# Late adaLN modulation by column groups with row-tile weight loads, and the shared expert's rows added on GpSimd at the end

## The reference, cut to what matters

```python
mod = silu(c) @ w_ada + b_ada                     # c: 1 + 8 conditioning rows; w_ada: 1024 x 6144
sh1, sc1, g1, sh2, sc2, g2 = split(mod, 6)
h = rms(x, norm_pre_mix) * (1 + sc1) + sh1
mix = concat(retention heads, gated-linear-attention (GLA) heads) @ w_out
x = x + g1 * rms(mix, norm_post_mix)
h = rms(x, norm_pre_ffn) * (1 + sc2) + sh2
f = routed_experts(h) + shared_expert(h)          # 64 experts, top 8 per token; one shared expert
y = x + g2 * rms(f, norm_post_ffn)
```

## Time and profile before

| | us |
|---|---|
| median of 3 runs (1336.25 to 1337.11) | 1336.88 |
| the profiled execution's own time | 1338.04 |
| its span, first to last instruction | 1335.8 |

### The profile page before, as it was taken

The page is one execution under the profiler, slowest core; times in us unless marked ns, Lnnn a source line. Parts: engine busy times, 40 slices in busy tenths (PEclk is TensorE's granted clock), DMA queues, the critical chain, the costliest instruction groups (busy, mean ns, idle before and its releaser), DMA issues.

```text
span 1335.8 us, 18616 instructions
## 1 busy us (share of the span) xinstructions
PE 1207.8 (90%) x5990; PEld 828.7 (62%) x5990; DVE 887.0 (66%) x1362; ACT 601.3 (45%) x712; POOL 163.4 (12%) x184
## 2 busy tenths in 40 slices
PE   5899999896899999999999999999999999999810
PEld 0799999754334244444777777777777777777500
DVE  0711442245465357575788888888888888888888
ACT  1422222203221012222677767767767767767501
POOL 0100000000011001101112212212212211221002
PEclk7799999986899999999999999999999999999955
DMA  9332221505135631537999999999999999999896
GB/s 372 138 112 74 74 74 37 130 0 189 63 126 170 230 129 39 142 119 264 355 380 395 389 383 385 378 376 382 375 369 374 377 378 381 374 379 359 348 318 221
DMA packets 91519, 339.20 MB, mean 254 GB/s; under 512 B 12312, under 2 KB 35880, under 8 KB 65420
## 3 DMA queue, kind: packets, MB, share of 16 engines
q1 hardware_dynamic: 75104, 301.02, 61.5%
q0 software_dynamic: 16384, 37.78, 8.1%
HBM read 317.24 MB, written 42.48 MB: 269 GB/s over the span
## 4 chain that ended last, share of the span: by engine, by line
PE 81%; DMA 8%; DVE 7%; ACT 2%; SPq 1%; issue 1%; DVEq 0%; POOLq 0%; POOL 0%; ACTq 0%
PE ps L1650 14%; PE ps L2033 13%; PE ps L2017 8%; PE ps L2013 7%; PE ps L2015 7%; PE ps L2014 7%; PE ps L1999 4%; PE ps L1863 4%; PE ps L1681 3%; DMA arena<-in_w_ada 3%; DMA arena<-expert_rows 2%; PE ps L1891 2%; PE ps L1912 1%; PE ps L1990 1%; PE ps L2023 1%
## 5 line engine op out<-in xcount | busy, mean ns | idle before, releaser
L1493 DVE TENSOR_TENSOR gu_lo<-w_gu,gu_hi 128x1536 fp32r<-128x1536 f32 x128 | 224.4, 1754 | 0.9 <-ACT gu_hi L1011 0.9
L1011 ACT ACTIVATE gu_hi<-w_gu 128x1536 fp32r<-128x1536 f32 x128 | 189.9, 1483 | 0.0
L1488 DVE TENSOR_TENSOR down_lo<-arena,down_hi 128x2048 fp32r<-128x2048 f32 x64 | 146.7, 2293 | 38.5 <-ACT down_hi L1017 38.5
L2013 PE MATMUL ps<-gu_hi,xT_hi 128*112 128x512 f32 x384 | 156.8, 408 | 0.9 <-issue 0.9
L2015 PE MATMUL ps<-gu_hi,xT_lo 128*112 128x512 f32 x384 | 151.2, 394 | 0.0
L2014 PE MATMUL ps<-gu_lo,xT_hi 128*112 128x512 f32 x384 | 150.8, 393 | 0.0
L1650 PE MATMUL ps<-w_hi,hT_hi 128*128 128x300 f32 (+1 forms) x480 | 145.0, 302 | 1.0 <-DVE w_lo L1093 1.0
L1650 PE MATMUL ps<-w_lo,hT_hi 128*128 128x300 f32 (+1 forms) x480 | 144.6, 301 | 0.0
L1650 PE MATMUL ps<-w_hi,hT_lo 128*128 128x300 f32 (+1 forms) x480 | 144.5, 301 | 0.0
L1017 ACT ACTIVATE down_hi<-arena 128x2048 fp32r<-128x2048 f32 x64 | 122.0, 1906 | 2.2 <-DMA arena<-in_w_exp_down 1.9
L2017 PE MATMUL ps<-w_gu,arena 128*112 128x512 f32 x256 | 120.2, 592 | 0.0
(11 more groups left out here) (271 smaller groups left out, 1932.1 us busy)
## 6 DMA issues: line engine op xcount, KB each, us to landing
w_gu<-in_w_exp_gate SPq DMA_DIRECT2D x64, 1024.0 KB, 10.3
w_gu<-in_w_exp_up SPq DMA_DIRECT2D x64, 1024.0 KB, 17.5
arena<-in_w_exp_down SPq DMA_DIRECT2D x64, 1024.0 KB, 12.7
arena<-in_w_ada SPq DMA_DIRECT2D x24, 1024.0 KB, 7.6
arena<-in_w_in SPq DMA_DIRECT2D x12, 1200.0 KB, 5.4
arena<-expert_rows SPq DMA_DIRECT2D x9, 1024.0 KB, 13.3
arena<-expert_rows SPq DMA_DIRECT2D x4, 2048.0 KB, 11.3
arena<-in_x_prompt SPq DMA_DIRECT2D x8, 512.0 KB, 8.7
```

The costliest lines, as they stand in the source:

```text
L1011: a.activation(gu_hi[b % RING][:, :, ks], w_gu[b % U][:, :, ks], ACT.Copy).then_inc(s_ghi, 1)
L1488: v.tensor_tensor(down_lo[:, :, :], w_dn[b % RING], down_hi[:, :, :].bitcast(F32), ALU.subtract).then_inc(s_dlo, 1)
L1493: v.tensor_tensor(gu_lo[b % U][:, :, ks], w_gu[b % U][:, :, ks], gu_hi[b % RING][:, :, ks].bitcast(F32), ALU.subtract).then_inc(s_glo, 1)
L2013: pe.matmul(out, x_hi, gu_hi[r][:, :, k], start=(k == 0), stop=False)
```

## The change

- The late modulation is tiled like the early one. Load `i` (0 to 15) brings row tile `k = i % 8` of half `g = i // 8`: 128 rows x 2048 columns, 8 KB a row. Four matmuls (`mod_piece`) write four column groups of one bank; the bias is four more matmuls a half. PE does 3, 3, 2, 3 and 3 pieces in the turns of the GLA loop and the last two behind it. Piece 8 waits until the first half has been folded.
- DVE folds twice, each time with two instructions of 64 partitions x 512: half 0 at the start of turn 3, half 1 behind the loop, ahead of `heads(PT)`. `mod_rows` becomes 256 rows x 512, and the loads back are in rows of 512 values. For each sample sequence there are two loads where there was one.
- `w_mod2` no longer uses the region ST0, and loads 2 and 3 don't wait for the store of the retention state.
- `w_out` is loaded in four parts. Row tiles 0, 1 and 6 (1.5 MB) are issued after the GLA states are stored, the others (2.5 MB) when the last GLA output has been copied. All `w_ada` loads are issued ahead of both.
- At the end DVE's addition of the shared rows is removed from `middle_ranks`. GpSimd does it, after the last scatter has landed and after `s_bcg`, and DVE waits for it ahead of its last addition.

```diff
-        w_mod2 = [region(at, 4, 512) for at in (MOD0 + 4 * D, HT0, HT0 + 2 * D, ST0)]
-        mod2 = region(MOD0, 8, 512, rows=NCOND)
+        w_mod2 = [region(at, 4, 512) for at in (MOD0 + 2 * D, MOD0 + 4 * D, HT0, HT0 + 2 * D)]
+        mod2 = region(MOD0, 2, 512)
+        MOD2_TURNS = (3, 3, 2, 3, 3)
...
+            def store_mod2(g):
+                sp.wait_ge(s_fold, 3 + g)
+                sp.dma_start(mod_rows[g * P:(g + 1) * P, :], mod2[:, g]).then_inc(s_mst, 16)
...
-            for i in range(1, 13):
+            for i in range(2, 12):
                 load_mod2(i)
+            store_mod2(0)
+            sp.wait_ge(s_out, 16)
+            sp.wait_ge(s_mst, 16)
+            sp.dma_start(bc2[:, 0:2]..., mod_row[0, 0:1].broadcast_to([P, 4, 512])).then_inc(s_bc2, 16)
+            for i in range(12, 16):
+                load_mod2(i)
             sp.wait_ge(s_sg, NCH)
...
+            load_w_out(0, 2)
+            load_w_out(6, 1)
             sp.wait_ge(s_goe, NT)
             sp.wait_ge(s_out, 16 * (1 + H))
-            sp.dma_start(w_out_buf, w_out[0].rearrange("(k p) n -> p k n", p=P)).then_inc(s_wout, 16)
-            for i in range(14, 16):
-                load_mod2(i)
+            load_w_out(2, 4)
+            load_w_out(7, 1)
+            store_mod2(1)
...
+            g.wait_ge(s_bcg, 16 * (1 + SB + 2))
+            for n, t in enumerate(LAST_ORDER):
+                R = ROWS[t]
+                g.wait_ge(s_add, t + 1)
+                g.tensor_tensor(ffn_sum[t][0:R], ffn_sum[t][0:R], shared[0:R, t], ALU.add).then_inc(s_tick, 1)
...
-                step(v.tensor_tensor(to, to, shared[0:R, t], ALU.add))
                 v.wait_ge(s_yb[t], 32)
                 step(v.tensor_tensor(y[:, 0], y[:, 0], y[:, 1], ALU.add))
+                v.wait_ge(s_tick, 1 + (done - NT))
                 mark(v.tensor_tensor(to, to, y[:, 0], ALU.add), s_add, done)
...
+            def mod_piece():
+                i = mod_pieces[0]
+                mod_pieces[0] += 1
+                g, k = i // KT, i % KT
+                pe.wait_ge(s_wada[i % 4], 16 * (i // 4 + 3))
+                if i == KT:
+                    pe.wait_ge(s_fold, 3)
+                for c in range(4):
+                    o = pe.matmul(ps[c * CG:c * CG + NCOND, MOD2_BANK], condT[:, k, :], w_mod2[i % 4][:, c], start=(k == 0), stop=False)
+                o.then_inc(s_ada, 1)
+                if k == KT - 1:
+                    pe.wait_ge(s_rows, 16 * 12)
+                    for c in range(4):
+                        o = pe.matmul(ps[c * CG:c * CG + NCOND, MOD2_BANK], K("selp")[c * CG:c * CG + 1, 0:NCOND], mod2_bias[c * CG:c * CG + 1, g],
+                                      start=False, stop=True)
+                    o.then_inc(s_mod, 1)
...
-            pe.wait_ge(s_fold, 2 + 5)
-            mod_mm(5)
-            mod_mm(6)
-            pe.wait_ge(s_goe, NT)
-            mod_mm(7)
+            while mod_pieces[0] < 2 * KT:
+                mod_piece()
```

More of the change, by code:

```diff
@@ L236, in hybrid_step @@
         mod1_bias = region(ST0 + 2 * D, 4, 512, rows=1)
[L237 to L240 removed]
+        w_mod2 = [region(at, 4, 512) for at in (MOD0 + 2 * D, MOD0 + 4 * D, HT0, HT0 + 2 * D)]
+        mod2 = region(MOD0, 2, 512)
+        mod2_bias = region(MOD0 + D, 2, 512)
+        MOD2_BANK = 2
+        MOD2_TURNS = (3, 3, 2, 3, 3)
         condT = sb("condT", [P, KT, NCOND])
@@ L551, in _ @@
                              state_gla[0, :, h].rearrange("b d v -> d b v")).then_inc(s_st, 16)
[L553 to L556, removed]
+            for c in range(4):
+                sp.dma_start(mod2_bias[c * CG:c * CG + 1], b_ada[0:1, 2 * D:6 * D].rearrange("a (g c n) -> a g c n", g=2, c=4)[:, :, c])\
+                    .then_inc(s_rows, 16)
+            for g, c, w in ((0, 0, norm_post_mix), (1, 0, norm_pre_ffn), (1, 2, norm_post_ffn)):
+                for half in range(2):
+                    sp.dma_start(mod2[(c + half) * CG:(c + half + 1) * CG, g], w[0:1, half * 512:half * 512 + 512].broadcast_to([CG, 512]))\
+                        .then_inc(s_rows, 16)
             def load_mod2(i):
@@ L1127, in _, with mod_fold @@
             v.wait_ge(s_const, 32)
[L1129 to L1134, removed]
-                    mark(v.tensor_copy(m, raw), s_fold, n + 3)
+            def mod_fold(g):
+                v.wait_ge(s_mod, g + 2)
+                v.wait_ge(s_rows, 16 * 12)
+                first, last = slice(0, 2 * CG), slice(2 * CG, P)
+                step(v.scalar_tensor_tensor(out=mod2[first, g], in0=ps[first, MOD2_BANK], scalar=float(g), in1=mod2[first, g], op0=ALU.add, op1=ALU.mult))
+                if g == 0:
+                    mark(v.tensor_copy(mod2[last, g], ps[last, MOD2_BANK]), s_fold, 3)
                 else:
-                    mark(v.scalar_tensor_tensor(out=m, in0=raw, scalar=one, in1=m, op0=ALU.add, op1=ALU.mult), s_fold, n + 3)
+                    mark(v.scalar_tensor_tensor(out=mod2[last, g], in0=ps[last, MOD2_BANK], scalar=0.0, in1=mod2[last, g], op0=ALU.add, op1=ALU.mult), s_fold, 4)
             def rotate(t):
@@ L1312, in _ @@
                     heads(t - 1)
-            mod_fold(4)
             head_squares(PT)
+            mod_fold(1)
             v_of_state(0)
             heads(PT)
-            for n in range(5, 8):
-                mod_fold(n)
             v.wait_ge(s_go, NT)
@@ L1802, in _ @@
                         o.then_inc(s_kv, 1)
-                        mod_part(t, 1 + c)
-                    mod_part(t, 3)
-                else:
-                    mod_part(t, 1)
-                    mod_part(t, 2)
-                    mod_part(t, 3)
+                        if c < MOD2_TURNS[t] - 1:
+                            mod_piece()
+                else:
+                    for n in range(MOD2_TURNS[t] - 1):
+                        mod_piece()
                 pe.wait_ge(s_gp, t + 1)
```

69 lines of the change are left out of this document (29 added, 40 removed).

## The result

The changed kernel takes 1319.33 us, the median of 4 runs (1313.46 to 1323.16), against 1336.57 us for the kernel before (4 runs): ratio 0.988, 95% interval 0.985 to 0.991. It is 17 us faster; 31 were forecast. The time lies at the upper end of the whole range (1295 to 1320) and outside the forecast's own (1300 to 1312), at the time of the rival "the clock stays low" (1320). The profiled execution took 1323.16 us, the longest of the four: span 1321.3, mean granted clock 0.920. The shortest, 1313.46, had 0.929. Medians and ranges here leave out three executions that took over 1.5% longer than the shortest of their kernel: 1599.03 of the kernel before, 1345.64 and 1348.22 of e10_fill_64_rows.

The account below looks back on a forecast made before the run. The chain of waits through PE and ACT, with modulation on it, was taken to bound the GLA loop and the gap behind. -16 - 21.6 + 1.7 + 1 + 4.1 = -30.8 from 1338.0 gave 1307.2, median 1306; range 1300 to 1312, whole 1295 to 1320.

Parts of the forecast that it names:

- the clock stays low: Rival, GLA loop: with modulation gone, PE's short matmuls and waits keep the clock low; 1320 us, chance 0.13.
- What one piece costs: Late modulation on PE: a piece of 8 records takes 1.07 us, or 1.94 at low clock, against 3.53 before.
- groups in series: Rival, modulation: four 9-column groups run one after another, a piece costs 3.53 us; 1346 if unhidden, chance 0.05.
- Turn by turn, -16: GLA loop: five turns save 4.7, 4, 3, 1 and 3.8 us, sum -16, range -20 to -11.
- The clock: GLA loop and behind: less modulation may leave more at 1.2 GHz; taken off in turns 1 and 2, 1.7 us added behind.
- Turn 3: GLA loop: PE sheds 3.5 us, but piece 8 waits for DVE's fold behind `heads(1)`; only 1 kept.
- The loads of `w_ada` don't decide: GLA loop: each load is asked for four pieces ahead, loads 12 to 15 a turn before they are needed.
- Behind the loop, -21.6: Last output copy to first output projection: 31.3 us become 9.6, with `w_out` the last to arrive; -21.6.
- The clock behind the loop, +1.7: Output projection: starting after a wait of some 2.7 us, it runs partly at low clock; +1.7 us.
- Loads back, +1: Samples' rows loaded back in 16 DMAs, not 8: between 2.7 us worse and 2 saved, taken as +1.
- The end: Final additions: GpSimd's five at 2.5 us go in turn with DVE's ten; +4.1 us, range -2.5 to +17.

Follow-up runs that it names:

- e10_fill_64_rows: Changed kernel plus zero-weight filler matmuls at 13 places, each four matmuls in four column groups, on 64 rows of PE: 1332.06 us, ratio 0.995.
- e3_fill: Changed kernel plus 13 zero-weight matmuls in one column group, two per GLA turn and three more ahead of the last outputs: 1310.82 us, ratio 0.982.
- e5: Changed kernel with 14 of the 16 modulation pieces written to column group 0 alone, so their matmuls run serially: 1321.68 us, ratio 0.989.
- e4: Changed kernel with `w_ada` loads 12 to 15 issued ahead of the modulation store and the 1 MB `bc2` load: 1323.44 us, ratio 0.988.
- e1: Changed kernel with the shared expert's rows added by DVE at the end, as before the change, not GpSimd: 1320.33 us, ratio 0.986.
- e7: Changed kernel plus zero-weight filler at 13 places, each four matmuls in four column groups, on 128 rows: 1310.06 us, ratio 0.981.
- e11: e7 with the shared expert's rows added by DVE at the end, as before the change: 1310.51 us, ratio 0.980.

## Why the prediction was wrong, point by point

**What one piece costs: right.** 1.05 or 1.89 us. The rival of groups in series is out.

**Turn by turn, -16: wrong, +4.0.** (The five terms make -16.5.) By turn, turn 0 from the first transposes to the first copy, the others copy to copy:

| turn | forecast | changed kernel | e3_fill |
|---|---|---|---|
| 0 | -4.7 | +0.9 | -2.6 |
| 1 | -4 | -1.9 | -6.8 |
| 2 | -3 | +1.4 | -4.8 |
| 3 | -1 | -2.0 | +2.5 |
| 4 | -3.8 | +5.5 | -1.9 |

Counted on a full clock the sum was right to 2 to 4 us (73 forecast; 75.4 and 76.7 with filler, which holds some of it itself). That is in part luck: the turns of e3 lie up to 3.5 off, in both directions. (In turn 2 the working leaves out the bias of the first half, which stands with piece 7 between the state products, so nothing was uncovered there.) What failed is the step called "The clock": "It was already at 0.63 in a 5 us stretch ... and came back when the modulation filled PE. With less of it more of the loop may run at 1.2 GHz; that is what I took off in turns 1 and 2." I took off about 2 us; it cost 18 in the profiled execution (93.0 against 75.4). The quoted sentence names the cause, and I didn't price it: each rise before came in or right behind a part of the modulation, 2.3 to 3.6 us of 128-row matmuls, and a new piece lasts 1.05 to 1.9. With most pieces made serial again (e5) the clock was back at 0.91. "Against: it came back each time" was no evidence against the rival, since the change shortens what it came back with. A chance of 0.13 for that rival was too low. That its 1320 was met is in part luck too: it has the loop at -4 (-16 and 12) and 2 us lost behind it, and measured were +4.0 and nothing; 6.5 us less ahead of the loop, in the middle and at the end made up for most of it.

**Turn 3: right in mechanism.** Piece 8 waited for DVE's fold (the chain shows L1159 ahead of 395.22). In e3 that wait is the largest one of the loop, 4.33, and the clock falls in it; there the turn is 2.5 longer than before, with 3.3 us of filler behind piece 8.

**"The loads of `w_ada` don't decide": wrong by 1.2 us, and by what followed.** Load 13 took 12.1 from issue to landing, behind the `bc2` load that SP issues ahead of it; in e4, where that load comes later, it took 5.2. I had counted what is queued behind the waiting SP and not what the broadcast load does to the loads behind it. The wait itself was 1.21; right at its end the clock fell, and it stayed low for turn 4, which ran 9.4 us shorter in the one profile of e4. The medians don't show that gain.

**Behind the loop, -21.6: right** (-20.6), with the releaser named: `w_out`, 9.26 from issue to landing.

**The clock behind the loop, +1.7: it did not come.** The output projection took 14.00 against 13.73 before; the start lost nothing that can be seen.

**Loads back, +1: too high by 1.** From the first issue to the landing of the last it is 14.1 for 14.0. The 2.65 that 8.97 gains on 11.62, counted from the last issue, went into the eight further issues, 2.7 as forecast.

**The end: right in mechanism, half in size.** In turn, as taken from the 1.39 against 0.56 of the earlier trace rows. 2.06 a GpSimd addition where I took 2.5; 5 x 2.06 + 10 x 1.26 = 22.9, from 1268.99 to 1291.8. The five are 2.2 shorter than forecast, and that is about what is missing from the 4.1 (by its own times, 1318.7 against 1314.4, the working gives 4.3). The rule of the Trainium skill's "SBUF — State Buffer", section "Who interferes with whom", holds here: DVE's addition takes 3.24 beside GpSimd's and 1.22 alone. The estimate of 2.25 from the Trainium skill's "GPSIMD Engine Reference", section "Elementwise — side-by-side cycle accounting", is nearer to the 2.06 than mine was.

**The sum.** Loop 20.0, gap 1.0, expert loop 1.8 against me; ahead of the loop 1.4, middle 3.2, end 1.9 for me: 16.3 of 16.3 (-30.8 forecast, -14.5 in the spans).

What stays open: why the clock held in turns 1 and 2 of e10 with the same filler under which it hadn't risen in turn 0; why the median of e10 is 13 us above the changed kernel's with a loop of the same length; and how much of a kernel's 10 us from run to run is this loop and how much lies ahead of it. Within the changed kernel, e1, e7 and e11 the longer executions have the lower mean clock (0.929 at 1311.97, 0.916 at 1326.39 in e1), but e3's longest, 1320.30, has 0.942, where its others have 0.938 to 0.945.

## What to carry to other kernels

When a change takes matmuls out of a stage in which the granted clock falls and comes back, ask what brings it back; if it is the work that goes, price the whole stage at 1.2 GHz, and that case is the first one and not a rival. A stage that is short of full-array matmuls can be faster with more of them: zero-weight matmuls into an open accumulation, at the heads of turns and ahead of waits, took 17.6 us off this loop in the profiles and 8.5 us off the median, and left its values alone. Additions moved from DVE to GpSimd, all with both operands in the SBUF, went in turn with DVE's here: DVE was rid of 1.26 us for each, GpSimd took an estimated 2.06 in its place, and the end came 2.2 to 2.7 later.

## What the runs showed of the hardware

- PE was busy throughout 340 to 350 at a granted clock of 0.50, with pieces in column groups among shorter matmuls; with two more such groups on 128 rows the clock was 0.83 there and then 1.00; with the same on 64 rows it was 0.50 in 350 to 360, with PE busy throughout.
- Matmul time and clock cancelled in this loop: 14 of 16 pieces at 3.6 or more with the clock at 0.91, and all at 1.05 to 1.9 with 0.59, give 91.4 and 93.0.
- Behind the issue (397.14) of the 1 MB load that spreads one row of 8 KB over 128 partitions, the DMA engines moved 151 GB/s in 400 to 402 and 129 in 402 to 404 at shares of 0.76 and 1.09, where the stretch 406 to 408 moves 419 at a share of 1.00. The four loads of `w_ada` behind it took 12.7, 12.1, 11.8 and 9.7 us from issue to landing; in e4_order, where they go ahead of it, 5.0, 5.2, 6.2 and 5.3.
- The samples' rows in 16 DMAs with rows of 2 KB, and in 8 with rows of 12 KB, took the same from the first issue to the last landing: 14.1 and 14.0 us.
